# The context's turning, its states and the bias tables moved from the mixing phase into the end of the projections, and idle products on TensorE behind the norms

## The reference, cut to what matters

```python
# first block
px = split(modulate(rms_norm(x), sh1, sc1) @ w_in)      # latent: NA q, k, v; HGRN2 q, f0, f1, i, g
pc = split(modulate(rms_norm(ctx), csh1, csc1) @ w_in)  # context: k, v; f0, f1, i
na = neighbourhood_attention(...)    # 8 heads: windows of 8 x 16 with a bias table, and 256 context keys
for d in range(2):                   # HGRN2, both directions
    _, s_c = gla_chunked(qc, k_c, vc, lf_c, 0, False)   # context: only its final state
    o, _ = gla_chunked(qx, k_x, vx, lf_x, s_c, True)    # latent scan starts from that state
x = x + gt1 * (concat(na, hg) @ w_out)
x = x + gt2 * peer_ffn(modulate(rms_norm(x), ...))      # product keys, 16384 experts, 8 x 16 chosen per token
x = rms_norm(x, norm_f)
# second block: rmsnorm, one wide projection, stick-breaking and latent attention, gates, w_out, final norm
```

## Time and profile before

| | |
|---|---|
| time, median of 3 runs | 2329.17 us (2326.9 to 2331.43) |
| the profiled execution's own time | 2327.29 us |
| its span, first to last instruction | 2325.5 us |
| PE busy | 2196.0 us, 94% of the span |
| DVE busy | 1664.4 us, 72% |
| ACT busy | 908.7 us, 39% |
| POOL busy | 624.9 us, 27% |
| mean granted TensorE clock | 0.977 of full |
| projections, mixing (start and end) | 0 to 285.3 us, 285.3 to 496.3 us |
| PEER, second block | 496.6 to 1833.4 us, 1833.7 to 2325.5 us |

### The profile page before, as it was taken

How to read it: one execution, slowest core, us unless ns; L and a number is a source line. 1 busy time by engine, 2 the same in 40 slices (tenths; PEclk the granted TensorE clock), 3 DMA queues, 4 the chain that set the end, 5 groups by cost and what they waited for, 6 DMA issues and landing times. The chain is left out here.

```text
span 2325.5 us, 31686 instructions
## 1 busy us (share of the span) xinstructions
PE 2196.0 (94%) x12605; PEld 1961.9 (84%) x12605; DVE 1664.4 (72%) x2779; ACT 908.7 (39%) x1191; POOL 624.9 (27%) x355
## 2 busy tenths in 40 slices
PE   5999889988999998999999899999999899889997
PEld 3888777866799998999999899999999777667775
DVE  6645677873479999889886788888887645656543
ACT  3322234343233333566663333333333434556432
POOL 0000042322347776333325333333332000000000
PEclk8999999999999999999999999999999999999999
DMA  7677400012237777899999999999998122111222
GB/s 263 216 235 240 163 33 1 1 73 73 91 115 244 248 241 235 314 357 339 353 356 385 356 359 352 358 355 352 359 353 308 68 82 90 55 42 55 78 90 73
DMA packets 177443, 486.13 MB, mean 209 GB/s; under 512 B 13648, under 2 KB 80336, under 8 KB 165776
## 3 DMA queue, kind: packets, MB, share of 16 engines
q1 hardware_dynamic: 140432, 349.87, 43.6%
q0 software_dynamic: 36864, 134.23, 15.5%
HBM read 429.52 MB, written 52.43 MB: 207 GB/s over the span
## 5 line engine op out<-in xcount | busy, mean ns | idle before, releaser
L1115 PE MATMUL ps<-h_high,u_high 128*128 128x384 f32 (+1 forms) x1216 | 427.7, 352 | 19.9 <-POOL u_low L1331 12.4
L1117 PE MATMUL ps<-h_high,u_low 128*128 128x384 f32 (+1 forms) x1216 | 419.7, 345 | 0.0
L1116 PE MATMUL ps<-h_low,u_high 128*128 128x384 f32 (+1 forms) x1216 | 419.6, 345 | 0.0
L1115 PE MATMUL ps<-w_high,v_high 128*128 128x384 f32 x1024 | 344.5, 336 | 7.5 <-DVE w_low L1750 7.5
L1117 PE MATMUL ps<-w_high,v_low 128*128 128x384 f32 x1024 | 343.8, 336 | 0.0
L1116 PE MATMUL ps<-w_low,v_high 128*128 128x384 f32 x1024 | 343.6, 336 | 0.0
L1115 PEld LDWEIGHTS ps<-h_high,u_high 128*128 128x128 f32 x1216 | 230.3, 189 | 33.9 <-POOL u_low L1331 14.6
L1481 ACT ACTIVATE v_high<-v_raw 128x2048 fp32r<-128x2048 f32 x64 | 122.6, 1916 | 347.9 <-PE ps L1117 341.2
L1115 PE MATMUL ps<-h_high,w_high 128*128 128x512 f32 x560 | 226.4, 404 | 17.1 <-DVE h_low L2422 5.1
L1117 PEld LDWEIGHTS ps<-h_high,u_low 128*128 128x128 f32 x1216 | 229.9, 189 | 8.0
L1116 PEld LDWEIGHTS ps<-h_low,u_high 128*128 128x128 f32 x1216 | 230.5, 190 | 7.1
(11 more groups left out here) (437 smaller groups left out, 4153.7 us busy)
## 6 DMA issues: line engine op xcount, KB each, us to landing
v_raw<-in_peer_v SPq DMA_DIRECT2D x64, 1024.0 KB, 6.4
w_raw<-in_w SPq DMA_DIRECT2D x94, 512.0 KB, 3.6
u_first<-in_uT SPq DMA_DIRECT2D x32, 1024.0 KB, 5.9
u_second<-in_uT SPq DMA_DIRECT2D x32, 1024.0 KB, 5.9
xT<-in_late_w SPq DMA_DIRECT2D x56, 512.0 KB, 4.4
gelu_up<-gelu SPq DMA_DIRECT2D x128, 192.0 KB, 6.3
gates<-gates_sb SPq DMA_DIRECT2D x12, 2048.0 KB, 9.9
weighted<-gelu_up SPq DMA_DIRECT2D x64, 384.0 KB, 6.7
```

Source lines behind the costliest of these rows:

```text
L1115: pe.matmul(out, wh, mh, start=start, stop=False)
L1116: pe.matmul(out, wh, ml, start=False, stop=False)
L1117: return pe.matmul(out, wl, mh, start=False, stop=stop)
```

## The change

The context's part leaves the mixing phase: `turn_context(0)` stands on PE behind the third last weight piece, `states(0)` and `turn_context(1)` behind the second last, `states(1)` behind the last, with their ACT copies. POOL adds bias tables 1 and 2 in the projections, once the context's jobs are done and the rows are loaded; DVE adds table 0 behind its last instruction there. Table 0, the turned keys and the states now lie in `k.xT`, tables 1 and 2 where the context's h lay. So SP loads `xT` only at the end of the mixing phase, behind the last item and the last read of a state, and `u_first` at its start. The steps in `fill` are 45 instead of 47.

In the other phases: `idle_products` (float32 matmuls of ones and zeros, 128x128 by 128x512, whose result nobody reads) stand on PE at the start of PEER (4), before and after its norm's spreading (2 and 2), and before and after that of the second block (3 and 3). The first group after PEER's norm does both tiles for each t. The last phase of PEER adds its squares later. The second block loads its first three weight pieces ahead of the positions, gives the low part of piece 1 to POOL, and runs its first two tiles in the order `FIRST_STEPS` of the projections.

```diff
@@ phase_project
+            pool.wait_ge(proj, ctx_done)
+            pool.wait_ge(k.table_in, 32)
+            for v in (1, 2):
+                off = TABLE_AT[v]
+                pool.tensor_tensor(k.bias[v].rearrange("p a h m -> p (a h) m"),
+                                   k.toep[:, :, :, off:off + KB].rearrange("p a h m -> p (a h) m"),
+                                   k.mask[:, v, :].unsqueeze(1).to_broadcast([P, ROWS * NH, KB]), ALU.add)
...
+            dve.wait_ge(k.table_in, 32)
+            off = TABLE_AT[0]
+            dve.tensor_tensor(k.bias[0].rearrange("p a h m -> p (a h) m"),
...
+                if p > turn_at[0]:
+                    d = p - turn_at[1]
+                    act.wait_ge(state_mm, d + 1)
+                    act.activation(k.state[:, d], ps[:, state_bank(d), :].rearrange("p (h t) -> p h t", t=P), ACT.Copy)
+                if p in turn_at:
+                    d = p - turn_at[0]
+                    act.wait_ge(turned_c, d + 1)
+                    for i, bank in enumerate(turn_banks(d)):
+                        last = act.activation(k.kcT[:, 4 * i:4 * i + 4, :], ps[:, bank, :].rearrange("p (i t) -> p i t", t=P), ACT.Copy)
+                    last.then_inc(turned_c_sb, 1)
...
+                if p > turn_at[0]:
+                    states(p - turn_at[1])
+                if p in turn_at:
+                    turn_context(p - turn_at[0])
@@ phase_mix
-    steps = [("ctx", d, 0) for d in range(2)]
+    steps = []
...
+            sp.dma_start(k.u_first[:], k.dram["w_out_g"][0]).then_inc(k.u_in[0], 16)
             xv = k.dram["xT"].rearrange("(k p) t -> p k t", p=P)
+            sp.wait_ge(maxed, 2 * N)
+            sp.wait_ge(av, HP * HG)
             for h in range(2):
                 sp.dma_start(k.xT[:, 4 * h:4 * h + 4, :], xv[:, 4 * h:4 * h + 4, :]).then_inc(k.load_x[h], 16)
-            sp.wait_ge(state_mm, 2)
-            sp.dma_start(k.u_first[:], k.dram["w_out_g"][0]).then_inc(k.u_in[0], 16)
@@ phase_peer
+def idle_products(pe, k, out, count):
+
+    for _ in range(count):
+        pe.matmul(out, k.ones[:], k.zeros[:], start=True, stop=True)
...
+            idle_products(pe, k, ps[:, 3, :], 4)
...
+            idle_products(pe, k, ps[:, 4, :], 2)
             pe.wait_ge(e_inverse, 1)
             spread_quarters(pe, k, ps[:, 6, :], rt[:]).then_inc(e_spread, 1)
+            idle_products(pe, k, ps[:, 4, :], 2)
...
+                if g == OUT_G:
+                    for j in range(GE):
+                        bank_free(GE * g + j)
+                    for t in range(KT):
+                        pe.wait_ge(h_split, OUT_TILES + t + 1)
+                        for j in range(GE):
+                            last = up_part(j, t)
...
-                if n >= 2:
+                if 2 <= n < KT - 2:
                     link(add_squares(n - 1))
+            for n in (KT - 3, KT - 2):
+                link(add_squares(n))
@@ second_block
-            sp.dma_start(pos_i[RS], k.dram["positions"].to_broadcast([2 * ROPE, T])).then_inc(rope_in, 16)
-            sp.dma_start(rope_cols[RS], k.dram["rope_cols"]).then_inc(rope_in, 16)
             for i in range(len(PIECES2)):
+                if i == RAWS:
+                    sp.dma_start(pos_i[RS], k.dram["positions"].to_broadcast([2 * ROPE, T])).then_inc(rope_in, 16)
+                    sp.dma_start(rope_cols[RS], k.dram["rope_cols"]).then_inc(rope_in, 16)
...
+            pool.wait_ge(w_high, 2)
+            pool.wait_ge(w_low, 1)
+            pool.tensor_tensor(wlo[:, 1, :], raw[:, 1, :], whi[:, 1, :].bitcast(F32), ALU.subtract).then_inc(w_low, 1)
...
+            idle_products(pe, k, ps[:, 3, :], 3)
             pe.wait_ge(n_inverse, 1)
             spread_quarters(pe, k, ps[:, 2, :], rt_q).then_inc(n_spread, 1)
-            for j in range(PROJECTED):
+            idle_products(pe, k, ps[:, 3, :], 3)
+            for j, steps in FIRST_STEPS:
+                if steps.start == 0:
+                    pe.wait_ge(w_low, j + 1)
+                for t in steps:
+                    if j == 0:
+                        pe.wait_ge(t_low, t + 1)
+                    last = first_part(j, t)
+                if steps.stop == KT:
+                    last.then_inc(tile_mm, 1)
+            for j in range(2, PROJECTED):
                 tile(j)
```

More of the change, by code:

```diff
@@ L539, in bank_free, with turn_context, states @@
                         pe.wait_ge(gated, silu_before[j - NB])
+            def turn_context(d):
+                pe.wait_ge(ctx_keys, 2)
+                for i, bank in enumerate(turn_banks(d)):
+                    bank_free(J + 3 * d + i)
+                    for n in range(4 * i, 4 * i + 4):
+                        h, j = divmod(n, 2)
+                        last = pe.transpose(ps[:, bank, n % 4 * P:(n % 4 + 1) * P], k.fc[d][:, h, j * P:(j + 1) * P], k.ident[:])
+                last.then_inc(turned_c, 1)
+            def states(d):
+                bank_free(J + 3 * d + 2)
+                pe.wait_ge(turned_c_sb, d + 1)
+                for h in range(HG):
+                    for j in range(2):
+                        last = pe.matmul(ps[:, state_bank(d), h * P:(h + 1) * P], k.kcT[:, 2 * h + j, :],
+                                         k.ic[:, j, h * P:(h + 1) * P], start=j == 0, stop=j == 1)
+                last.then_inc(state_mm, 1)
             for p, steps in FIRST_STEPS:
@@ L752, in values @@
                 last.then_inc(summed, 1)
[L754 to L767, removed]
             def level(unit, s):
@@ L774, in level @@
                     pe.wait_ge(kk_ready, unit + 1)
-                    if unit == 0:
-                        pe.wait_ge(state_mm, 2)
-                    elif unit % 2 == 0:
+                    if unit and unit % 2 == 0:
                         pe.wait_ge(hg_out, HP * (unit // 2))
@@ L816, in read_out @@
                 pe.wait_ge(off_cp, 2 * unit + 2)
-                if unit == 0:
-                    pe.wait_ge(state_sb, 2)
-                elif d == 0:
+                if unit and d == 0:
                     pe.wait_ge(hg_out, HP * (unit // 2))
@@ L992, in level @@
                 if 10 * unit + s - 1 < 2:
-                    if unit == 0 and s == 1:
-                        dve.wait_ge(state_mm, 2)
                     dve.tensor_tensor(q, k.hq[:, H, :], pre, ALU.mult).then_inc(q_ready, 1)
@@ L2536, in build @@
                 k.hgate = sb("hgate", [P, HG, T], where=na)
+                with ExitStack() as parts:
+                    k.hc = [sb(name, [P, KT, C], F32R, where=parts) for name in ("hc_high", "hc_low")]
+                tables = sb("bias", [P, 2, ROWS, NH, KB], where=na)
+                spare = k.xT[:].rearrange("p a t -> p (a t)")
+                k.bias = [spare[:, 0:2048].rearrange("p (a h m) -> p a h m", a=ROWS, h=NH), tables[:, 0], tables[:, 1]]
+                k.kcT = spare[:, 2048:3072].rearrange("p (n d) -> p n d", d=P)
+                k.state = spare[:, 3072:4096].rearrange("p (e h t) -> p e h t", e=2, h=HG)
                 phase_project(k)
```

91 lines of the change are left out of this document (36 added, 55 removed).

## The result

The changed kernel takes 2334.72 us (median of 20 runs, 2329.53 to 2340.63), the kernel before 2331.16 (20 runs beside them, 2325.16 to 2333.53). The ratio is 1.0019 (95%: 1.0013 to 1.0026). The interval leaves out no change, but the difference is smaller than the 0.2% that the prediction took as its limit.

A forecast was written before the change was run, and what follows sets the result against it. PE bounds (94% busy), sharing the mixing with DVE. Gains -6.0 + 10.3 + 0 + 4.9 + 0.6 + 0.2 = 10.0 us off 2327.3 give 2317.3; plus 1.9 to the median and 0.8 for clock: 2320, range 2313 to 2327.

The forecast's parts named there:

- Projections' end: End of the projections: context work between PE's weight pieces, 3.7, and DVE's table 0, 2.3, make it 6.0 us longer.
- Mixing: Mixing phase: 14.1 us of its slow start goes, less 1.6 for POOL's `kd` and 2.2 for two items: 10.3 us shorter.
- the mixing is PE's: Rival, mixing phase: items cost whole slots on PE, so it wins only 3.9 us; 2325.6 us; chance 0.12.
- the clock falls in the new waits: Rival: half clock after PE's waits at w_out's tile 6, second block's tile 3, mixing's start; 2325 us; chance 0.13.
- Start of PEER: Start of PEER: full clock wins at most 0.4 us, a late second-weights load may cost up to 3; taken as 0.
- The slower rival: Rival, start of PEER: `u_second`'s load behind `xT` lands 10 us late and delays all behind it; 2330 us; chance 0.05.
- PEER's norm: PEER's norm and the group behind it: spreading at full clock and two tiles side by side, 4.9 us shorter.
- Taken back in PEER's long stretch: Rival, PEER's long stretch: DVE, busy 58.55 of 60 us, takes back the 4.9; 2324 us; chance 0.08.
- Second block: Second block's start: earlier weights, full clock and the new tile order, less a hold on DVE beside POOL: 0.6 us shorter.
- The prediction's own sign of being wrong: Signs named beforehand: mixing longer than 203 us, half clock in the group behind the norm, or POOL's tables reaching the barrier.
- "Slower": Whole kernel: the outcome beyond the limit of 0.2% (4.7 us) on the slower side; chance 0.05.

The follow-up runs named there:

- e1: The changed kernel with every recurrence step back in the slot it had in the kernel before; 2321.39 us, ratio 0.9954 to the kernel before.
- e5: e1, with DVE making table 0 behind its casts for the masks instead of behind its last gate; 2321.96 us, ratio 0.9969 to the kernel before.
- e9: The kernel before with only the recurrence steps of units 1 to 3 moved to the changed kernel's slots; 2343.72 us, ratio 1.0062.
- e6: e1, with the two xT loads issued right behind the load of the second weights, not ahead; 2323.42 us, ratio 0.9968 to the kernel before.
- e7: e1 without any of the idle products; 2325.84 us, ratio 0.9978 to the kernel before.
- e8: e1, with DVE instead of POOL making the second weights' low part in the second block; 2318.78 us, ratio 0.9954 to the kernel before.
- e3: The changed kernel with unit 1's read-out and unit 2's first two levels one slot later; 2329.44 us, ratio 0.9991 to the kernel before.

## Why the prediction was wrong, step by step

- **Projections' end, 6.0.** 6.4 measured in the changed kernel, 5.8 in e1. The parts are right, and the stage's own spread is over 1 us; the 2.3 for table 0 is worth only 1.2 if taken away (e5), since the last state's copy comes next.
- **Mixing, -10.3: the step that failed.** It was priced as if the slots stayed ("everything up to 300.16 but `kk` goes", then two items more), and +1.8 came. The work removed was priced about right: with the slots restored the mixing is 9.0 to 10.6 us shorter in six profiles. What failed is that I took the removed list entries for free. They were places in an order, and their going moved two steps off their cover: 10.8 us by e1's stage, and 13.3 slower by e9 where they are moved alone (3.4 of it at a place that the change doesn't have).
- **The rival "the mixing is PE's" (items cost whole slots)** is not what happened either: e1 has the same items and work and is 10.8 shorter. The rival "the clock falls in the new waits" named the mechanism, but not the places that cost. Of its three only the mixing's start had a half clock in after (298.2 to 301.7, 0.51), and before has that there too (286.7 to 293.5, 0.50; 303.7 to 307.1, 0.51). The falls at 397 and 445 lie in gaps that I had not foreseen.
- **Start of PEER, 0 (from -3 to 0.4).** 0.8 us longer; e6 shows the load as the cause. The mechanism was in the text, its timing off at one point: SP's `xT` loads went out at 503.26, behind the wait for the last read-out, and `u_second` at 504.76, so that both were under way together and `u_second` took 9.4 us; I had them issued from about 495. The slower rival had the right place, but ACT waited 0.9 us for the load, not ten.
- **PEER's norm, -4.9.** -4.6; the group took 11.0 where 10.9 was worked out. e7 puts 2.0 of it to the idle products; the rest is the order of the tiles and the spreading's clock, by the traces.
- **Taken back in PEER's long stretch:** no. It took 1242.3 against 1242.4.
- **Second block, -0.6.** +0.9, and 0.3 to 1.8 over the profiles with the same code. The hold on DVE was 2.2 us (2.91 against 0.74) and PE waited 1.73 us for `low(3)`, both as foretold. The step that failed here is that `low(3)` would end 0.5 us later: it came 1.9 later, since `low(2)` waits for ACT, and ACT for the end of tile 0, which now comes 1.9 later. So tile 3 started 0.7 us later behind the last sum, not 0.6 earlier. The rule of the Trainium skill ("SBUF — State Buffer", section "Who interferes with whom") agrees with that 2.91, and the 2.5 us that the edit would have given without it didn't come. What the hold costs is open: e8 put work of about its length in its place.
- **A number that came near by luck.** With the slots restored e1's median is 2321.39, close to the 2320 forecast. By stages it gives 6.7 us, not 10.0 (9.0 - 5.8 - 0.8 + 4.6 - 0.3).
- **What the chances missed.** The prediction's own sign of being wrong, a mixing longer than 203 us, did show: 213.7. "Slower" had 0.05 and hung on one mechanism; the plain question which steps stand side by side after the change was not asked.

## What to carry to other kernels

Where an order comes from a rule over indices (spread over slots, interleaving, due times), removing or adding an entry is a change to all of it: write out both orders and compare them place by place before pricing anything. For each producer that stands close ahead of its consumer on the engine that bounds, ask what lies between them now, and price a gap as the wait plus the half clock behind it. And judge a change by its parts: here a good half hid behind a bad line, and moving that line turned 4 us of loss into 10 of gain.

## What the runs showed of the hardware that was not expected

- PE needn't be idle for long to lose its clock: behind waits of 3.0 and 2.85 us, and behind one of 3.17, the granted clock was 0.52 and 0.51, of the level of 1.2 GHz. But the spreading behind a wait of 1.74 us took 1.16 us in e7, where the kernel before took 1.78 us behind the same wait; in e7 the half clock showed only in the group behind it. And from 293 to 307 us the same steps ran at a mean of 0.52 in e3 and 0.88 in after, which cost e3 1.1 us. So where the clock falls, and for how long, differs between runs of the same code.
- So profiles of the same code differ: PEER's long stretch took 1239.6 to 1244.5 us and the last stage 369.8 to 373.3 over twelve profiles. A difference of a few us between two single profiles must be placed in a stage before it is believed.
- What a DVE product loses beside POOL's is POOL's remainder. In the changed kernel it came 1.89 us behind POOL's start (518.05 - 516.16) and took 3.23; in e6 2.91 behind (506.44 - 503.53) and took 2.25. It ended 0.55 us behind POOL's in both: 516.16 + 4.57 = 520.73 against 521.28, 508.14 against 508.69. Where DVE's product started first it was POOL's that was held: in e1 it took 2.83 us (1830.73, DVE's at 1830.60), in after 2.34.
